# Two transformer blocks on one Trainium2 core: the modulation vectors computed on VectorE instead of GpSimd and TensorE

## The chip, the cores and the metric

One core of a Trainium2 chip (trn2) runs the whole program in one launch. The metric is the device time of one execution in microseconds. Five engines work side by side, each through its own queue in order: TensorE (PE, with its weight loads shown as PEld), VectorE (DVE), ScalarE (ACT), GpSimd (POOL) and SyncE (SP), which only issues DMAs here. They wait for one another by semaphores.

## The reference, cut to what matters

Two blocks, each of two layers. The first runs on 272 tokens (256 and 16 meta tokens), the second on 512 (256 and 256 of a context). In the second block every sublayer is wrapped by a modulation: a vector for each of two streams, made once from a condition by a matrix product, which shifts, scales and gates each sublayer.

```python
def ada_in(h, g, m, j):                       # m: the modulation of a layer and stream
    xn = rms_norm(h, g)
    return (xn * (1.0 + m[:, j, 1][:, None]) + m[:, j, 0][:, None]).astype(h.dtype)

def gated_residual(h, m, j, y, w):
    return h + (w * m[:, j, 2][:, None] * y).astype(h.dtype)
```

For each layer and each of two streams the vector has 9 x 1024 values: `silu(c) @ w_mod + b_mod`, with c of 1024 values, so 9216 outputs a layer, 144 tiles of 128 outputs in both layers. `w_mod` of both layers is 75 MB, read once.

## The kernel before, in words

All large products are cut in panels of weights, 128 x 1024 floats (512 KB), 632 of them, in one list that is walked in order. A panel lands in one of four slots of `raw` (SP, L370, issued when the panel four places back is used up), is split in a high part `whi` (ACT, L1078) and a low part `wlo` (DVE, L1642), and TensorE multiplies each of its eight 128 x 128 pieces three times (L484 to L486: high by high, low by high, high by low). `split` and `next_panel` do this on ACT and DVE: after each finished panel (`panel_done`) one further panel is split, three panels ahead of TensorE. The results go to PSUM banks 0 to 3 in turn, and `bank_free` gives them back.

Block 1 (layers 0 and 1): norm, input projection, attention of three kinds with panels between its steps as fillers, merge, a feed-forward of 32 panels in and 32 panels out. Layer 1 of it works on 256 columns. Block 2: a SwiGLU (44 panels in, 22 out), retention (16 panels of queries and keys, token tiles, heads, 16 panels out), SwiGLU, SwiGLU, neighbourhood attention, SwiGLU. Each sublayer ends in `residual`: 8 output tiles m = 0 to 7, each added to `h` by DVE (`update`), then a norm. Between residual and norm, called a boundary below, TensorE sums squares (L599, L606), ACT takes the root (L1122), DVE the reciprocal and four diagonal tiles (L1679, L1682), TensorE spreads them (L612), and DVE and ACT write the normed input chunk by chunk (L1719, L1142, L1708), which TensorE's first three tiles follow (L525, L526, L530).

The modulation is computed beside this in 36 groups of 512 outputs:

- POOL (`mod_group`, L389 to L437) reads the weights with the input dimension on the partitions. For a group it loads four pieces of 128 x 1024 (L436), multiplies each half by the condition's value of each partition (`tensor_scalar`, L400) and adds it up in `macc` (`tensor_tensor`, L402), 30 steps a group, each waiting for the one before. It then waits until TensorE has read `macc` (`mod_done`), and at four groups until the norm's low parts are written (`POOL_HOLD`).
- TensorE (`mod_group`, L504 to L512) sums `macc` over the partitions by 8 products with a tile of ones, of 64 columns each. It stands at fixed places in TensorE's program, given by the tables at L83 to L85: after a unit, after the spreads and after two heads of the stick-breaking attention; inside the residual, between panels of the feed-forwards, and in five boundaries (`mod_norm`), between L606 and L612.
- DVE (`mod_tiles`, L1741) adds the bias and writes `modv`, a bank of PSUM to each group.
- `modulations` turns the scale part into gains `gsc` and halves the gates.

POOL also stores the bias tables of the neighbourhood attention by column (L445), one after each of the last 16 groups but one, and later fills `bia` from them.

## Time and profile before

| | us |
|---|---|
| median of 3 runs | 3238.52 |
| lowest, highest | 3232.12, 3242.91 |
| span of the profiled execution | 3230.1 |
| PE busy | 3136.0 (97%) |
| DVE busy | 1724.8 (53%) |
| ACT busy | 1270.9 (39%) |
| POOL busy | 1950.4 (60%) |

The span runs from the first to the last instruction of the profiled execution. Its own time outside the span isn't recorded; the median of the runs shown is 8.4 us above the span. Busy time of PE hides its clock: a matmul at half clock counts as busy for longer.

### The profile page before, as it was taken

To read this page: it belongs to the slowest core of one execution; us is meant where nothing else is said; L and a number is where in the kernel's file an instruction comes from. 1 tells how busy PE (TensorE), PEld (TensorE's weight loads), DVE (VectorE), ACT (ScalarE), POOL (GpSimd) and SP (SyncE) were. 2 spreads that over 40 slices of the span, in tenths; PEclk is the share of its full clock that TensorE was granted. 3 is DMA by queue.
4 is the path that set the end of the run, shared out by engine and by line. 5 is a ranking of instruction groups with operands and counts; after the bars stand their busy time and mean duration, and the time that the engine had idled before them with its cause. 6 is when DMAs were issued, how large, how long until landed. Compare 5 with 4: busy or idle time off the path is not lost.

```text
span 3230.1 us, 48616 instructions
## 1 busy us (share of the span) xinstructions
PE 3136.0 (97%) x18046; PEld 2660.2 (82%) x18046; DVE 1724.8 (53%) x2409; ACT 1270.9 (39%) x2132; POOL 1950.4 (60%) x1285
## 2 busy tenths in 40 slices
PE   7999899999999999999999999999999999999998
PEld 6677899976779998888887777888888888886898
DVE  5665776655668865443435465544435443436554
ACT  4445555343555643222232443322223222235443
POOL 6658477514994975677567658678875777603000
PEclk9999999999999999999999999999999999999999
DMA  5323455632335663333443223334433443332354
GB/s 195 111 92 105 138 189 194 204 105 95 112 117 168 215 210 121 122 126 122 134 130 117 85 85 108 119 129 130 136 125 110 133 138 125 123 119 76 131 182 156
DMA packets 120280, 430.35 MB, mean 133 GB/s; under 512 B 13857, under 2 KB 17185, under 8 KB 119729
## 3 DMA queue, kind: packets, MB, share of 16 engines
q1 hardware_dynamic: 93632, 335.24, 31.7%
q0 software_dynamic: 24576, 86.46, 8.4%
q10 hardware_dynamic: 1904, 6.36, 0.5%
q8 instruction: 113, 1.85, 0.2%
q14 instruction: 55, 0.44, 0.1%
HBM read 426.95 MB, written 8.85 MB: 135 GB/s over the span
## 4 chain that ended last, share of the span: by engine, by line
PE 86%; POOL 5%; DVE 3%; ACT 2%; DMA 2%; issue 2%; ACTq 0%; DVEq 0%; SPq 0%; POOLq 0%
PE ps L484 22%; PE ps L486 21%; PE ps L485 21%; PE ps L511 2%; PE ps L581 2%; PE ps L582 2%; PE ps L583 2%; POOL macc L402 2%; DMA raw<-in_panels 2%; POOL modraw L400 2%; POOL mprod L400 1%; PE ps L525 1%; PE ps L530 1%; PE ps L526 1%; PE ps L986 1%
## 5 line engine op out<-in xcount | busy, mean ns | idle before, releaser
L1642 DVE TENSOR_TENSOR wlo<-raw,whi 128x1024 fp32r<-128x1024 f32 x632 | 856.0, 1355 | 914.6 <-ACT whi L1078 889.5
L1078 ACT ACTIVATE whi<-raw 128x1024 fp32r<-128x1024 f32 x632 | 668.4, 1058 | 1417.2 <-PE ps L486 901.2
L484 PE MATMUL ps<-xhi,whi 128*128 128x512 f32 (+2 forms) x2792 | 949.3, 340 | 3.1 <-DVE wlo L1642 2.5
L486 PE MATMUL ps<-xhi,wlo 128*128 128x512 f32 (+2 forms) x2792 | 934.6, 335 | 0.0
L485 PE MATMUL ps<-xlo,whi 128*128 128x512 f32 (+2 forms) x2792 | 933.7, 334 | 0.0
L484 PEld LDWEIGHTS ps<-xhi,whi 128*128 128x128 f32 x2792 | 531.8, 190 | 70.8 <-issue 14.8
L485 PEld LDWEIGHTS ps<-xlo,whi 128*128 128x128 f32 x2792 | 531.8, 190 | 51.8 <-issue 1.9
L486 PEld LDWEIGHTS ps<-xhi,wlo 128*128 128x128 f32 x2792 | 531.4, 190 | 50.2
L400 POOL TENSOR_SCALAR modraw<-modraw,cs 128x512 f32<-128x512 f32 x288 | 552.1, 1917 | 27.6
L400 POOL TENSOR_SCALAR macc<-modraw,cs 128x512 f32<-128x512 f32 x36 | 70.5, 1958 | 745.2 <-PE ps L511 602.5
L400 POOL TENSOR_SCALAR mprod<-modraw,cs 128x512 f32<-128x512 f32 x252 | 445.8, 1769 | 19.0 <-POOL macc L402 0.2
L402 POOL TENSOR_TENSOR macc<-macc,mprod 128x512 f32<-128x512 f32 x252 | 360.3, 1430 | 21.0
L402 POOL TENSOR_TENSOR macc<-macc,modraw 128x512 f32<-128x512 f32 x216 | 336.8, 1559 | 17.5
L484 PE MATMUL ps<-ghi,whi 128*128 128x512 f32 (+1 forms) x704 | 255.8, 363 | 0.0
L486 PE MATMUL ps<-ghi,wlo 128*128 128x512 f32 (+1 forms) x704 | 255.5, 363 | 0.0
L485 PE MATMUL ps<-glo,whi 128*128 128x512 f32 (+1 forms) x704 | 255.4, 363 | 0.0
L486 PEld LDWEIGHTS ps<-ghi,wlo 128*128 128x128 f32 x704 | 133.0, 189 | 20.6
L484 PEld LDWEIGHTS ps<-ghi,whi 128*128 128x128 f32 x704 | 133.0, 189 | 20.5
L485 PEld LDWEIGHTS ps<-glo,whi 128*128 128x128 f32 x704 | 133.0, 189 | 20.4
L2183 DVE TENSOR_TENSOR sq<-tmp,ps 128x512 f32<-128x512 f32 (+1 forms) x88 | 54.6, 620 | 175.1 <-PE ps L486 174.4
L484 PE MATMUL ps<-fhi,whi 128*128 128x272 f32 (+1 forms) x512 | 146.4, 286 | 0.3 <-DVE wlo L1642 0.3
L486 PE MATMUL ps<-fhi,wlo 128*128 128x272 f32 (+1 forms) x512 | 146.2, 286 | 0.0
(362 smaller groups left out, 4752.9 us busy)
## 6 DMA issues: line engine op xcount, KB each, us to landing
raw<-in_panels SPq DMA_DIRECT2D x632, 512.0 KB, 3.3
modraw<-in_mod POOLq DMA_DIRECT2D x144, 512.0 KB, 4.4
bias_by_column<-in_rpb POOLq DMA_DIRECT2D x16, 476.2 KB, 8.3
bia<-bias_by_column POOLq DMA_DIRECT2D x32, 96.0 KB, 2.6
rtab<-in_rtab ACTq DMA_DIRECT2D x2, 1312.0 KB, 7.4
wuq<-in_wuq ACTq DMA_DIRECT2D x2, 768.0 KB, 6.7
con<-in_con SPq DMA_DIRECT2D x1, 1345.5 KB, 13.7
h<-in_x SPq DMA_DIRECT2D x1, 1088.0 KB, 6.7
```

The source lines that it names most:

```text
L400: pool.tensor_scalar(out, a, b, None, op).then_inc(mod_step, 1)
L402: pool.tensor_tensor(out, a, b, op).then_inc(mod_step, 1)
L484: pe.matmul(out, w_hi, x_hi, start=start, stop=False)
L485: pe.matmul(out, w_hi, x_lo, start=False, stop=False)
L486: return pe.matmul(out, w_lo, x_hi, start=False, stop=stop)
L511: last = pe.matmul(bank(b, o, o + SUM_W), macc[:, s * 512 + j * P:s * 512 + (j + 1) * P], ones[:, 0:SUM_W], start=True, stop=True)
L581: pe.matmul(out, xh, wh(4 * kk, 512), start=(k == 0), stop=False)
L582: pe.matmul(out, xl, wh(4 * kk, 512), start=False, stop=False)
L583: last = pe.matmul(out, xh, wl(4 * kk, 512), start=False, stop=(k == NC - 1))
L1078: act.activation(whi[:, s * PW:(s + 1) * PW], raw[:, s * PW:(s + 1) * PW], ACT.Copy).then_inc(hi_split, 1)
L1642: dve.tensor_tensor(wlo[:, s * PW:(s + 1) * PW], raw[:, s * PW:(s + 1) * PW], whi[:, s * PW:(s + 1) * PW].bitcast(F32), ALU.subtract).then ...
L2183: dve.tensor_tensor(w_, v, bank(b, 0, T), ALU.mult).then_inc(bank_free[b], 1)
```

## The change

The weights of the modulation are laid out the other way round, with the output on the partitions: tile k holds 128 outputs and half a row, 512 of the 1024 input values (128 x 512, 256 KB, 288 such halves). The condition (both streams) is read to every partition (`cb`, 128 x 2048, a new DMA on SP), and ACT takes its silu there after the first norm. DVE multiplies a half by `cb` and sums along the row in one `tensor_tensor_reduce` for each stream; the second half starts from the sum of the first. After two tiles (four halves) DVE adds the bias and writes `modv`. POOL only issues the loads, two slots of 256 KB, each when the half in it is used up, and the bias tables' stores. TensorE's groups, their banks and the tables of places are gone.

The halves stand behind panels on DVE (`mod_half` after `next_panel`): 16 in each residual of block 1's feed-forward; in block 2 one behind each panel of three SwiGLUs (64 each), two behind each of the 16 panels of retention's queries and keys, one behind each of the 16 panels of its residual, and one behind each of the first 16 panels of the neighbourhood attention. `modulations` is now called just ahead of each norm, and the gates are halved ahead of the residual.

```diff
-AW = 23552
+AW = 24576
...
+            sp.dma_start(cb[:, :], t["cond"].broadcast_to([P, 2 * D])).then_inc(cond_in, 16)
...
+            n_halves = 2 * DEPTH * MODT
+            for k in range(n_halves):
+                s = k % 2
+                if k >= 2:
+
+                    pool.wait_ge(mod_step, 2 * (k - 1) + (k - 2) // 4)
+                pool.dma_start(modraw[:, s * MOD_W:(s + 1) * MOD_W], t["mod"][k, :, :]).then_inc(mod_landed[s], 16)
+                hh = (k - n_halves) // 8 + NH
+                if hh >= 0 and k % 8 == 7:
...
-                if mod:
-                    mod_group()
...
-                if c == 0:
-                    act.wait_ge(const_in, 32)
-                    act.activation(cs[:, :], par[:, P_C:P_C + 2 * NC], ACT.Silu).then_inc(silu_c, 1)
-                elif c == 4:
+                if c == 4:
                     split()
             for layer in range(DEPTH):
 
                 norm(T1, between=first_chunks if layer == 0 else None)
+                if layer == 0:
+                    act.wait_ge(cond_in, 16)
+                    act.activation(cb[:, :], cb[:, :], ACT.Silu).then_inc(silu_c, 1)
...
+            def mod_half():
+
+                j = mod_count.slot(4)
+                half, m = j % 2, j // 2
+                landed, done = lane.count(mod_landed[half]), lane.count(mod_step)
+                landed.add(16)
+                if mod_count.reg is None and mod_count.static == 0:
+                    dve.wait_ge(silu_c, 1)
+                dve.wait_ge(mod_landed[half], landed.value())
+                for s in range(2):
+                    w = modraw[:, half * MOD_W:(half + 1) * MOD_W]
+                    if done.reg is not None or done.static > 1:
+                        dve.wait_ge(mod_step, done.value(1))
+                    c = modsum[:, 2 * m + s:2 * m + s + 1]
+                    at = s * D + half * MOD_W
+                    dve.tensor_tensor_reduce(w if s else modprod[:, :], w, cb[:, at:at + MOD_W], 1.0, c if half else 0.0, ALU.mult, ALU.add,
+                                             modsum[:, 4 + 2 * m + s:5 + 2 * m + s] if half else c).then_inc(mod_step, 1)
+                    done.add(1)
...
+                        if mod and mod(m, e):
+                            mod_half()
...
+                residual(16, T2, add2(0, 1), mod=lambda m, e: True)
...
+                for i in range(16):
+                    next_panel()
+                    lane.tile.add()
+                    mod_half()
```

TensorE at the boundary from block 1 to block 2. Before:

```order
L486 MATMUL ps<-fhi,wlo 128x256
L599 MATMUL ps<-con,tmp 128x64 x4
L606 MATMUL ps<-con,sq 128x64 x4
L511 MATMUL ps<-con,macc 128x64 x8
L612 MATMUL ps<-sq,con 128x128 x4
L525 MATMUL ps<-xhi,whi 128x512
```

After, where L532 and L536 are the former L606 and L612:

```order
L428 MATMUL ps<-fhi,wlo 128x256
L525 MATMUL ps<-con,tmp 128x64 x4
L532 MATMUL ps<-con,sq 128x64 x4
L536 MATMUL ps<-sq,con 128x128 x4
L457 MATMUL ps<-xhi,whi 128x512
```

The eight products of the group are gone from between the sums of squares and the spreads; the same holds at four more boundaries.

DVE at the end of retention's residual, last output tile. Before:

```order
L1642 TENSOR_TENSOR wlo<-raw,whi 128x1024
L2166 SCALAR_TENSOR_TENSOR h<-ps,modv,h 128x256 x2
L1642 TENSOR_TENSOR wlo<-raw,whi 128x1024
L2208 SCALAR_TENSOR_TENSOR gsc<-modv,par 128x16
L2211 TENSOR_SCALAR modv<-modv 128x16
L1679 RECIPROCAL small<-small 128x4
```

After (`ISA` is the product with its sum, the `ISA` of 128x1 the read of the sum):

```order
L1654 ISA modprod,modsum<-modraw,cb,modsum 128x512
L1654 ISA modsum 128x1
L1654 ISA modraw,modsum<-modraw,cb,modsum 128x512
L1654 ISA modsum 128x1
L1662 TENSOR_TENSOR modv<-modsum,par 128x4
L2078 SCALAR_TENSOR_TENSOR h<-ps,modv,h 128x256 x2
L1547 TENSOR_TENSOR wlo<-raw,whi 128x1024
L2127 SCALAR_TENSOR_TENSOR gsc<-modv,par 128x16
```

One half, with the write of `modv`, now stands between the last panel and the last update of `h`.

DVE in the 16 panels of retention's queries and keys had 15 `wlo` in a row before. After:

```order
L1547 TENSOR_TENSOR wlo<-raw,whi 128x1024
L1654 ISA modprod,modsum<-modraw,cb 128x512
L1654 ISA modsum 128x1
L1654 ISA modraw,modsum<-modraw,cb 128x512
L1654 ISA modsum 128x1
L1654 ISA modprod,modsum<-modraw,cb,modsum 128x512
L1654 ISA modsum 128x1
L1654 ISA modraw,modsum<-modraw,cb,modsum 128x512
L1654 ISA modsum 128x1
L1547 TENSOR_TENSOR wlo<-raw,whi 128x1024
```

Two halves, four products with sums, stand between two `wlo`.

## Rows read from the trace of the kernel before

**Rows 1.** The page: busy us, share of the span and instructions of each engine
```profile
PE 3136.0 (97%) x18046; PEld 2660.2 (82%) x18046; DVE 1724.8 (53%) x2409; ACT 1270.9 (39%) x2132; POOL 1950.4 (60%) x1285
```

**Rows 2.** Groups by line, TensorE's modulation products: count, busy us, mean ns, idle before
```profile
L511 PE MATMUL ps<-con,macc 128*128 128x64 f32 x576 | 72.8, 282 | 4.5 <-POOL macc L402 3.8 <-ACT v L1511 0.7
```

**Rows 3.** The chain that ended last, in time: start us, us, what; some L511 pieces
```profile
919.95 2.94 PE ps L511 x16
...
1082.33 1.97 PE ps L511 x16
...
1152.97 1.73 PE ps L511 x16
...
1322.94 1.73 PE ps L511 x16
...
1390.05 1.73 PE ps L511 x16
```

**Rows 4.** Timeline of the boundary into block 2: start us, us, engine, line, idle before
```profile
1226.28 1.11 PE L606 MATMUL ps<-con,sq 128*128 128x64 f32 x8 [2.57 <-ACT sq L1116]
...
1228.09 0.88 DVE L1682 TENSOR_SCALAR sq<-con,small 128x128 f32<-128x128 f32 x4
...
1229.99 2.02 PE L612 MATMUL ps<-sq,con 128*128 128x128 f32 x8
...
1250.52 0.58 ACT L1460 ACTIVATE tmp<-ps 128x512 f32<-128x512 f32 x1
```

**Rows 5.** Timeline of the boundary into retention
```profile
1603.94 1.11 PE L606 MATMUL ps<-con,sq 128*128 128x64 f32 x8 [0.83 <-ACT sq L1116]
...
1605.69 0.87 DVE L1682 TENSOR_SCALAR sq<-con,small 128x128 f32<-128x128 f32 x4
1606.67 1.11 PE L612 MATMUL ps<-sq,con 128*128 128x128 f32 x8
...
1623.87 0.58 ACT L1485 ACTIVATE qk<-ps 128x512 f32<-128x512 f32 x1
```

**Rows 6.** Timeline of the boundary of layers 0 and 1, without a group
```profile
630.03 0.68 DVE L1682 TENSOR_SCALAR sq<-con,small 128x128 f32<-128x128 f32 x3
630.37 1.47 PE L612 MATMUL ps<-sq,con 128*128 128x128 f32 x6 [0.98 <-DVE sq L1682]
```

**Rows 7.** Windows of 2 us: busy PE, PEld, DVE, ACT, POOL; granted clock, DMA share, GB/s
```profile
632.00:634.00 2.00, 1.01 (x4) 1.04 (x5) 1.88 (x5) 0.96 (x3) 0.00 (x0) 0.50 0.66 256
...
1230.00:1232.00 2.00, 2.00 (x9) 1.72 (x9) 0.65 (x2) 0.28 (x1) 0.00 (x0) 0.50 0.00 0
...
1610.00:1612.00 2.00, 2.00 (x10) 1.67 (x9) 1.97 (x5) 0.91 (x2) 0.00 (x0) 1.00 0.01 5
```

**Rows 8.** DVE's groups by form in 2090 to 2430 us (POOL at work), then 3000 to 3230 (idle)
```profile
L1642 DVE TENSOR_TENSOR wlo<-raw,whi 128x1024 fp32r<-128x1024 f32 x62 | 86.6, 1397 | 132.1 <-ACT whi L1078 132.1
...
L1642 DVE TENSOR_TENSOR wlo<-raw,whi 128x1024 fp32r<-128x1024 f32 x71 | 87.0, 1225 | 87.2 <-ACT whi L1078 85.7 <-PE ps L486 1.4
```

**Rows 9.** Timeline of DVE: the only product-like operation with a sum, neighbourhood attention
```profile
2926.54 0.68 DVE L2372 CUSTOM_DVE_ANT_1 nsc<-ps,bia 128x512 f32<-128x512 f32 x1
2927.15 0.08 DVE L2372 DVE_READ_ACCUMULATOR2_ANT small<- 128x1 f32 x1
2927.15 0.69 DVE L2372 CUSTOM_DVE_ANT_1 nsc<-ps,bia 128x512 f32<-128x512 f32 x1
```

**Rows 10.** DMA issues: KB each, median us to landing; then the line L436 by itself
```profile
raw<-in_panels SPq DMA_DIRECT2D x632, 512.0 KB, 3.3
modraw<-in_mod POOLq DMA_DIRECT2D x144, 512.0 KB, 4.4
...
DMA to landing us min/median/max: 3.4/4.3/7.0
```

**Rows 11.** Waits of TensorE: us in total, times, longest
```profile
PE ps L765 <- DVE att L2062: 6.6, 4, 2.6
```

**Rows 12.** Timeline of the start: ACT's table load ahead of the silu
```profile
14.89 1.28 ACT L1179 ACT_TABLE_LOAD   x1
```

More of the change, by code:

```diff
@@ L502, in new_bank @@
                 return b
-            def mod_group():
-                b = new_bank()
-                lane.take(mod_step, MS)
-                for j in range(4):
-                    for s in range(2):
-                        o = (2 * j + s) * SUM_W
-                        last = pe.matmul(bank(b, o, o + SUM_W), macc[:, s * 512 + j * P:s * 512 + (j + 1) * P], ones[:, 0:SUM_W], start=True, stop=True)
-                last.then_inc(mod_done, 1)
             def first_tiles(T, w, count=FIRST, middle=None):
@@ L1305, in _ @@
                 filler(15)
-                lane.tile.add()
                 for hh in range(MH):
@@ L1409, in _ @@
                 lane.count(part_lo).add(NC)
-                residual(NC, T, mod_after=MOD_OUT, gain=layer * PL + P_LN2)
+                residual(NC, T, gain=layer * PL + P_LN2)
                 def relu(i):
@@ L1452, in shifts, with swiglu @@
                 return of
-            def swiglu(layer, j, T, norm_=None, mod=False, mod_after=()):
-                norm(T, shifts(layer, j, T), then=ACT.Silu, mod=mod)
+            def swiglu(layer, j, T):
+                norm(T, shifts(layer, j, T), then=ACT.Silu)
                 def pair(i):
@@ L1465, in pair @@
                     act.activation(col(ghi, i, T2, T), sq[:, (b // 2) * T2:(b // 2) * T2 + T], ACT.Copy).then_inc(part_hi, 1)
-                for part, (at, n) in enumerate(parts(2 * FF2, MOD_TILES2 if mod else ())):
-                    lane.tile.add(part > 0)
-                    with lane.loop(n // 4, [(lane.panel, 4), (lane.split, 4), (lane.tile, 4)]) as i:
-                        pair(i * 2 + at // 2)
-                        pair(i * 2 + (at // 2 + 1))
-                residual(FF2, T, norm_, mod_after)
+                with lane.loop(2 * FF2 // 4, [(lane.panel, 4), (lane.split, 4), (lane.tile, 4)]) as i:
+                    pair(i * 2)
+                    pair(i * 2 + 1)
+                residual(FF2, T)
             def block2():
                 lane.take(mod2_ready)
-                swiglu(0, 0, T2, None, True, MOD_FF2)
+                swiglu(0, 0, T2)
                 act.dma_start(rtab[:, :], t["rtab"]).then_inc(rtab_in, 16)
-                norm(T2, shifts(0, 1, T2), mod=True)
+                lane.take(mod2_ready)
+                norm(T2, shifts(0, 1, T2))
                 def qk_copy(i0):
@@ L1745, in residual @@
+            def residual(K, T, update, norm_=None, mod=None, between=None, gain=None):
                 norm_ = T if norm_ is None else norm_
@@ L2123, in _ @@
                 merged_lo(NC // 2 - 1)
-                residual(NC, T, add1, mod_after=MOD_OUT, gain=L + P_LN2)
+                residual(NC, T, add1, gain=L + P_LN2)
                 wait_tiles(lane)
@@ L2145, in _ @@
                 step(dve.tensor_copy(rs[:, 0:T], bank(5, 0, T)))
-                residual(FF1, T, add_folded, T1 if layer < DEPTH - 1 else T2, MOD_FF, between=decay_logs if layer == 0 else None)
+                residual(FF1, T, add_folded, T1 if layer < DEPTH - 1 else T2, mod=lambda m, e: m < NC - 1 and (e % 2 == 0 or (e == 1 and m < 2)), between=decay_logs if layer == 0 else None)
                 wait_tiles(lane)
@@ L2189, in pair @@
                     lane.count(part_lo).add()
-                for part, (at, n) in enumerate(parts(2 * FF2, MOD_TILES2 if mod else ())):
-                    if part:
-                        mod_tiles()
-                    with lane.loop(n // 4, [(lane.panel, 4), (lane.split, 4), (lane.tile, 4), (lane.count(part_hi), 2), (lane.count(part_lo), 2)]) as i:
-                        pair(i * 2 + at // 2)
-                        pair(i * 2 + (at // 2 + 1))
+                    if mod:
+                        mod_half()
@@ L2196, in swiglu @@
+                four = [(mod_count, 4), (lane.count(mod_landed[0]), 32), (lane.count(mod_landed[1]), 32), (lane.count(mod_step), 9)] if mod else []
+                with lane.loop(2 * FF2 // 4, [(lane.panel, 4), (lane.split, 4), (lane.tile, 4), (lane.count(part_hi), 2), (lane.count(part_lo), 2)] + four) as i:
+                    pair(i * 2)
+                    pair(i * 2 + 1)
                 lane.settle(part_lo)
-                residual(FF2, T, add2(layer, j), norm_, mod_after)
+                halves(layer, j)
```

253 lines of the change are left out of this document (81 added, 172 removed).

## The prediction, made blind

> **What bounds the kernel now.** I read the page first: TensorE is busy for 3136.0 of 3230.1 us, DVE for 1724.8, POOL for 1950.4 [rows 1]. So the end is set by TensorE's own queue nearly everywhere, and an edit is worth what it takes out of that queue or adds as a wait to it. Of TensorE's work I looked up the part that the change removes: 576 products at L511, busy for 72.8 us together, with 4.5 us of idle time in front, 3.8 of it for POOL's `macc` [rows 2]. POOL's 1950.4 us themselves cost next to nothing: it waits for TensorE, not the other way. The chain that ended last shows one group of L511 as one piece of 1.73 us at full clock, longer (up to 2.94) where the clock was low or POOL late; there are 36 such groups, 31 in line with other products and 5 at boundaries [rows 3]. The same rows give TensorE's pace: from 1322.94 to 1390.05 lie 12 panels and one group, so a panel of 512 columns takes 5.45 us; from 1082.33 to 1152.97 lie 24 panels of 256 columns, 2.86 us each [rows 3].
>
> **What is removed from TensorE, in line.** 29 of the 31 groups stand in a full queue: 29 x 1.73 = 50.2 us [rows 3]. The other two stand at the end of the stick-breaking attention of each layer, took 2.2 and 2.94 us and waited about 1.4 us each for POOL, 8.0 in all. A little behind them TensorE waits for the softmax of the differential attention on DVE (L765, up to 2.6 us a time, 6.6 in all [rows 11]), so arriving earlier partly lengthens that wait. Bounds 0 and 8.0; I take half, 4.0.
>
> **At the boundaries** the group stood where TensorE would wait for the diagonals anyway. Without a group the spreads start 0.34 us after the first diagonal was begun, 630.03 to 630.37 [rows 6]. With one, L612 started at 1229.99 where 1228.09 + 0.34 was possible [rows 4], 1.56 us late, and at 1606.67 where 1605.69 + 0.34 was possible [rows 5], 0.64 late. Five boundaries lie between 3.2 and 7.8 us; I take 5.0, the middle, since two had the long form.
>
> **DVE and POOL part company.** In the SwiGLU with POOL at work a `wlo` takes 1397 ns, at the end of the program with POOL idle 1225 [rows 8]. After the change POOL computes nothing until the neighbourhood attention. Where DVE hides behind TensorE that gives nothing; in attention, where TensorE waits for DVE's chains [rows 11], it may give 0 to 6.6 us. I take 2.0.
>
> Removed in all: 50.2 + 4.0 + 5.0 + 2.0 = 61.2 us.
>
> **What is added on DVE.** 288 halves of two products with a sum, each product followed by a read of the sum. The trace has one such operation, with one input in PSUM: the next starts 0.61 us after it, the read of 0.08 us inside that time [rows 9]. A half is then 2 x 0.61 and some 0.2 for the last read and the waits, 1.4 to 1.5 us; 288 of them 430 us. In a SwiGLU, a panel gives DVE 5.45 us, of which `wlo` takes 1.2, the product and the low part of a tile pair 0.7 a panel (two operations of 128 x 512 for two panels, 0.68 each as in [rows 9]), and the half 1.5: 3.4 of 5.45. With two halves behind a panel it is 1.2 + 3.0 = 4.2 of 5.45. In the first 8 panels of the neighbourhood attention it is 1.2 + 1.5 = 2.7 of 2.86, just enough; in block 1's residuals, two or three halves on four panels, about the same. Behind the waiting half on DVE stands the next `wlo`, and for that TensorE waits. The cover is the lead of three panels: at 2.86 us 8.6 us, less a panel's way of 3.3 for landing [rows 10], 1.2 for `whi` (twice the 0.58 of 512 columns [rows 4]) and 1.2 for `wlo`, leaves about 3 us; at 5.45 more. So the products are hidden, with bounds 0 and what the rivals below give; I take 1.0 for small stalls in the tight stretches.
>
> At one place there is no cover. In retention's residual the last half stands between the last panel and the last update of `h`, on the path to the norm: 1.4 us and the write of `modv` (0.1 to 0.2). **1.5 us**, once.
>
> **The loads.** A slot is filled again when its half is used up. A load of 512 KB from POOL lands after 3.4 to 7.0 us, median 4.3 [rows 10]; the new ones are 256 KB, so 4.3 is a cautious value. One half a panel at 5.45 us: two panels, 10.9 us, for 1.5 + 4.3. Two halves a panel: 5.8 for 5.45, a lag of 0.35 a panel, 5.6 us in 16 panels, mostly inside the lead. At 2.86: 5.8 for 5.72. Covered, by the 1.0 above. The bias stores stay behind loads of halves at the SwiGLU's pace and end with the last half, before the panels of values that come ahead of the first score with a bias; I count nothing.
>
> **The start.** The silu of `cb` on ACT is now 2048 columns wide: a table load of 1.28 [rows 12] and four times 0.58 [rows 4], 3.6 us behind the norm, just where ACT should split panel 3. TensorE has two panels of work then, so between 0 and 3.6 reach it; I take 1.2. The silu of 16 columns that goes had stood beside DVE's work.
>
> **The clock at the boundaries.** At the boundary into block 2, after an idle time of 2.57 us ahead of L606 [rows 4], the granted clock went to 0.50 (1.2 GHz); at the one into retention, with 0.83 idle [rows 5], it stayed at 1.00 (2.4 GHz) [rows 7]. From the spreads to the first evacuated tile it took 20.53 us there [rows 4] and 17.20 here [rows 5]: a fall costs 3.3 us. Of the five boundaries with a group three had fallen already; so had the one of layers 0 and 1, which has no group and only short gaps (clock 0.50 at 632 [rows 7]). After the change the two that held lose the group that filled their gap; the one behind retention's residual gets 1.5 us of idle time on top. I take both as falling: 6.6 us, bounds 0 and 6.6.
>
> **The sum.** 61.2 - 1.0 - 1.5 - 1.2 - 6.6 = 50.9 us less, a span of about 3179 instead of 3230.1. The profiled execution lies 8.4 us below the median of the runs shown, a distance that stays, so 3238.5 - 50.9 = 3187.6, rounded to **3187 us**, 1.6% faster.
>
> **Rivals.**
>
> *The gaps don't cost the clock and attention gains* (chance 0.18). No further fall (+6.6), the two late groups in full (+4.0), more relief of DVE in attention: 61 to 68 us less, about 3173. For it: the clock held at two of five; against: no boundary without a group held.
>
> *The product with a sum takes twice as long with both inputs in SBUF* (0.08). No row shows that form; `wlo`, with both in SBUF and no sum, runs at 1.2 ns an element [rows 8], the same as the summing form with one in PSUM [rows 9], which speaks against it. A half is then 2.7 us. Two a panel: 5.4 + 1.2 = 6.6 for 5.45, 1.2 x 16 = 18.4 us; at 2.86: 1.04 x 8 = 8.3; block 1's residuals some 7; the uncovered half 1.2; less about 12 for the lead of four stretches: 23 us lost, 3211. This is what a page of the Trainium skill would have: "Vector Engine (DVE) Microarchitecture Reference", section 7, says that the scalar-tensor-tensor shape loses half its throughput when both sources come from SBUF and aren't bf16, since no read port is left for the accumulator. I can't tell whether it holds for this operation, so it speaks against the change for 23 us only.
>
> *Attention takes back its groups* (0.08). Eight groups stand there; if TensorE waits for DVE and ACT right behind all of them, about 12 us more are lost and it is 3199.
>
> *The halves land late* (0.06), the case that ends slower. DVE waits in order for a load, the `wlo` behind it is late, and TensorE stands still. With L from issue to landing, a pair of slots turns in 1.5 + L. Lost: 16 (1.5 + L - 5.45) in the queries and keys, 10 times (1.5 + L - 5.72) in the neighbourhood panels and block 1's residuals, less 12 for the lead. At L = 7.0, the longest of before [rows 10], that is 65 us: 3252, slower than before. From L = 6.5 on it eats the whole gain. For it: these stretches carry the panels beside, at 2.86 us 512 KB each or 183 GB/s; against: median 4.3 for twice the size.
>
> *The change does nothing* isn't open: TensorE's 72.8 us of L511 are gone for certain; they could only come back as waits, as above.
>
> **Chances and range.** The forecast with its own spread, 3177 to 3198, 0.60; the fast rival 0.18; attention 0.08; double time 0.08; late halves 0.06, half of that beyond the old time. The range holds the forecast, attention, most of the fast rival and the double time: 3168 to 3212. About 0.3%, 10 us, is what a measurement of this kernel can tell from no change. Faster by more than that: 0.94; within it 0.02; slower 0.04.
>
> **What would show it.** No L511 and a TensorE busy time near 3080 us. At the five boundaries the spreads 0.34 us after the first diagonal, and a clock of 0.50 for 8 to 10 us at all of them. A product with a sum of 0.61 to 0.69 us (1.2 would be the second rival), DVE's busy time near 1930 us, that is 1724.8 and 576 x 0.65 more, less some 170 (632 `wlo` and the other forms with both inputs in SBUF, each up to 0.17 shorter [rows 8]). `wlo` near 1225 throughout. In the queries and keys and in the first neighbourhood panels, waits of DVE for the loads below 1 us. Wrong would be: waits of TensorE for `wlo` of more than 5 us in these stretches, or an unchanged clock at the boundaries with a gain above 60 us.

## The result, and the profile after

The changed kernel takes **3154.59 us** (median of 4 runs, 3153.55 to 3155.57) against 3239.43 us (4 runs, 3232.12 to 3242.91) for the kernel before on the same chip: a ratio of 0.9739, 95% interval 0.9722 to 0.9756. It is 2.6% faster, 84.8 us. The forecast was 3187 us with a range of 3168 to 3212: the right sign, and a gain that is two thirds larger than forecast. The page of the changed kernel, as [rows 1]:

```profile
span 3151.8 us, 48239 instructions
PE 3061.4 (97%) x17470; PEld 2586.3 (82%) x17470; DVE 1865.4 (59%) x3597; ACT 1272.4 (40%) x2132; POOL 204.6 (6%) x349
```

The 576 group products of [rows 2] are gone from TensorE, and POOL is down from 1950.4 to 204.6 us. DVE has 141 us more. The products by the tile that they write, half of all (the other half writes `modraw` and has the same durations), with DVE's waits ahead of them:

```profile
engine op xcount: duration ns min/median/max, first and last start us, forms
L1654 DVE CUSTOM_DVE_ANT_0 modprod<-modraw,cb x144: 680/684/694, 511.8 to 2815.1; 128x512 f32<-128x512 f32 x144
L1654 DVE CUSTOM_DVE_ANT_0 modprod<-modraw,cb,modsum x144: 742/746/752, 515.0 to 2823.9; 128x512 f32<-128x512 f32 x144
...
  DMA modraw<-in_mod: 31.0, 28
```

A product with both inputs in SBUF takes 0.68 us, as the nearest row of before with one input in PSUM did [rows 9]; where the sum is carried on from the first half of the row it takes 0.75. DVE waited 31.0 us in all for a half to land, 22.4 of them at 1570 to 1660 us, in retention's queries and keys, where two halves stand behind each panel (us in total, times, longest):

```profile
DVE modprod L1654 <- DMA modraw<-in_mod: 22.4, 20, 2.2
```

TensorE hardly felt it: all its waits for `wlo` at L426 in the whole run are 3.8 us. The loads, as [rows 10]:

```profile
raw<-in_panels SPq DMA_DIRECT2D x632, 512.0 KB, 3.5
modraw<-in_mod POOLq DMA_DIRECT2D x288, 256.0 KB, 3.0
```

And DVE in the SwiGLU at 2030 to 2370 us, as [rows 8]; `wlo` is down from 1397 to 1226 ns, the value that before had only with POOL idle:

```profile
L1547 DVE TENSOR_TENSOR wlo<-raw,whi 128x1024 fp32r<-128x1024 f32 x64 | 78.4, 1226 | 96.7 <-ACT whi L992 95.5 <-issue 1.0
```

**Where the 78.3 us of span went.** Both kernels issue the same 17,470 other products on TensorE in the same order, so each product of after can be set beside its twin of before, and the distance between them, read along the program, is a ledger of the gain. It jumps by 1.70 to 1.73 us at 25 of the 29 groups in line. At two, those behind the spreads of the latent attention (190.7 and 805.2 us before), it jumps by 0.5 only: TensorE then waits for DVE's `att` instead, 1.45 us each time. At two others it jumps by 2.9 and 2.7, since TensorE had also waited there before (0.9 us for POOL's sum, 0.7 for ScalarE). And there is one entry nobody had asked for:

| Entry (us of span, gain positive) | Forecast | Measured |
|---|---|---|
| 29 groups in line | 50.2 | 49.3 |
| 2 late groups of the stick-breaking attention | 4.0 | 7.7 |
| 5 groups at boundaries | 5.0 | 4.8 |
| Differential attention and merge, beside its groups | 2.0 | **17.4** |
| Small stalls | -1.0 | -1.1 |
| Uncovered half behind retention's residual | -1.5 | -1.5 |
| Start | -1.2 | +0.8 |
| Clock at the boundaries into retention and behind it | -6.6 | -5.2 |
| Wait for `wlo` in retention's rope | 0 | 2.0 |
| The rest: 0.06 to 0.13 us right behind each group in line (2.5 together), 0.7 more at the boundary ahead of neighbourhood attention, small pieces | 0 | 4.1 |
| Span | 50.9 | 78.3 |

At the boundary ahead of neighbourhood attention the clock was at 0.50 for 13.7 us before and 3.4 after, and that gave next to nothing: with the clock up TensorE waits there for DVE's `xlo`, 0.37 us at a time and once 0.85. The wait in the rope is DVE relieved of POOL once more: its twelve operations took 13 us before and 8 after, and a wait of 1.88 us for `wlo` went.

The other 6.5 us of the 84.8 are not in this ledger, which compares one execution of each kernel: the span profiled before lies 9.3 us below the median time of that kernel, the one profiled after 2.8 below. In the changed kernel and in e1 to e10 the time is 1.7 to 2.0 us above the span, so the profile of before caught a fast execution.

### The profile page after: what moved, and what is told of

Its sections match the earlier page's. It is cut to its first block and busy times, and to the rows that moved or that the text cites. A ratio compares the mean times of both kernels' runs of the same rounds, so it can differ in the third digit from the quotient of the medians.

```text
span 3151.8 us, 48239 instructions
## 1 busy us (share of the span) xinstructions
PE 3061.4 (97%) x17470; PEld 2586.3 (82%) x17470; DVE 1865.4 (59%) x3597; ACT 1272.4 (40%) x2132; POOL 204.6 (6%) x349
## 5 line engine op out<-in xcount | busy, mean ns | idle before, releaser
L1547 DVE TENSOR_TENSOR wlo<-raw,whi 128x1024 fp32r<-128x1024 f32 x632 | 773.5, 1224 | 730.5 <-ACT whi L992 694.6
L426 PE MATMUL ps<-xhi,whi 128*128 128x512 f32 (+2 forms) x2792 | 945.5, 339 | 4.3 <-DVE wlo L1547 3.8
L426 PEld LDWEIGHTS ps<-xhi,whi 128*128 128x128 f32 x2792 | 529.4, 190 | 73.1 <-issue 15.4
L384 POOL DMA_DIRECT2D modraw<-in_mod x288 | 155.1, 539 | 2643.6 <-DVE modsum L1654 2457.6
L426 PE MATMUL ps<-ghi,whi 128*128 128x512 f32 (+1 forms) x704 | 255.2, 362 | 0.0
L426 PEld LDWEIGHTS ps<-ghi,whi 128*128 128x128 f32 x704 | 132.9, 189 | 20.8
L426 PE MATMUL ps<-fhi,whi 128*128 128x272 f32 (+1 forms) x512 | 146.1, 285 | 0.1
L427 PE MATMUL ps<-flo,whi 128*128 128x272 f32 (+1 forms) x512 | 145.8, 285 | 0.0
L507 PE MATMUL ps<-whi,xhi 128*128 128x512 f32 (+1 forms) x288 | 116.5, 405 | 2.6 <-ACT qk L1392 1.8
L508 PE MATMUL ps<-whi,xlo 128*128 128x512 f32 (+1 forms) x288 | 114.6, 398 | 0.0
L509 PE MATMUL ps<-wlo,xhi 128*128 128x512 f32 (+1 forms) x288 | 114.5, 397 | 0.0
```

The lines of the kernel that those rows point to most:

```text
L384: pool.dma_start(modraw[:, s * MOD_W:(s + 1) * MOD_W], t["mod"][k, :, :]).then_inc(mod_landed[s], 16)
L426: pe.matmul(out, w_hi, x_hi, start=start, stop=False)
L427: pe.matmul(out, w_hi, x_lo, start=False, stop=False)
L507: pe.matmul(out, xh, wh(4 * kk, 512), start=(k == 0), stop=False)
L508: pe.matmul(out, xl, wh(4 * kk, 512), start=False, stop=False)
L509: last = pe.matmul(out, xh, wl(4 * kk, 512), start=False, stop=(k == NC - 1))
```

## The experiments

Ratios are to the kernel before on the same chip, with 95% intervals. Runs e1 to e4 shared their runs of before (3241.1 us), so did e5 to e8 (3241.2), and e9 and e10 (3241.4). The stretch that most of them are about is the differential attention with its merge, once in each layer of block 1, between the same two products of TensorE in every kernel. Windows over it: us, then busy time of PE, PEld, DVE, ACT and POOL (instructions), mean granted clock, DMA share, GB/s. The kernel before:

```profile
310.14:411.50 101.36, 92.81 (x650) 84.81 (x650) 71.69 (x140) 54.00 (x116) 52.06 (x34) 0.93 0.41 139
922.90:1021.20 98.30, 89.88 (x650) 82.08 (x651) 72.34 (x139) 53.21 (x116) 50.63 (x34) 0.92 0.43 140
```

The changed kernel:

```profile
301.24:394.34 93.10, 89.70 (x649) 82.72 (x648) 64.65 (x140) 54.68 (x118) 0.00 (x0) 0.96 0.39 128
891.08:980.21 89.13, 84.06 (x649) 77.06 (x648) 63.12 (x138) 53.37 (x118) 0.00 (x0) 0.98 0.40 134
```

8.26 and 9.17 us less, 17.4 together. TensorE's idle time (the length less PE's busy time) fell by 5.15 and 3.35 us, 8.5 together. Its busy time fell too, for the same products, since the clock was at 0.50 for 13.3 and 15.1 us of them before and for 6.8 and 3.4 after: 18.2 us less at half speed, 9.1 us less lost. 8.5 and 9.1 are 17.6, the whole of it. DVE was busy 7.0 and 9.2 us less for the same operations. By place, TensorE's idle time fell by 5.1 us at the products that transpose `att` (L765), by 2.5 where it waits for DVE's gates and by 1.1 where it waits for `mlo`; its waits for ScalarE did not shrink.

How steady is such a stretch? The second profile of the changed kernel (e10 below) has 91.24 and 90.82 us for the same two, 1.9 less and 1.7 more, by where the clock fell; the sum is 182.06 against 182.23. In e8, whose edit changes nothing up to the end of these stretches, the sum is 185.7. So 3 us of a sum can come with no edit at all, and before has one profile only.

**Theory A:** POOL's arithmetic had held up DVE, and DVE's chain is what TensorE waits for here. **Rival B:** POOL's loads of 512 KB did. **Rival C:** the groups did, by their banks and their places.

**e1 and e2: POOL's arithmetic put back.** Into the changed kernel, in the two stretches and in part of the attention ahead of them, POOL gets work on two spare tiles that nobody reads; e1 alternates these two, e2 has writes alone:

```
+            if i % 2: pool.tensor_tensor(spare[0], spare[0], spare[1], ALU.add)
+            else:     pool.tensor_scalar(spare[1], spare[0], 1.0, None, ALU.mult)
...
+            pool.memset(spare[i % 2], 0.0)
```

> The changed kernel, with idle work put on POOL in both attentions of block 1: 140 operations of 128 x 512 each that read a spare tile and write one (tensor_scalar and tensor_tensor in turn, as the old kernel had them), over the stretches in which POOL had worked before; nothing else is changed. Theory A, DVE's operations with two inputs in SBUF were held up by POOL's reads and TensorE waited for DVE in the differential attention: the two stretches (310 to 413 and 923 to 1023 us before) get back most of the 17 us that they gained, the span rises by 12 to 20 us, wlo's mean in these stretches goes from 1225 to near 1400 ns, and half-clock time of TensorE there goes from 10 towards 28 us. Theory B, the loads of the modulation had disturbed the panels: no change (within 3 us). Theory C, the groups on TensorE cost more than their 1.73 us in the attention: no change.

> The changed kernel, with POOL kept busy in the same places by 420 memsets of 128 x 512 each, which write SBUF and read nothing. Theory A in the narrow form (POOL's reads hold DVE up): within 3 us of the changed kernel, wlo stays near 1225 ns. Theory A in the wide form (any work of POOL): slower by 10 us or more, like the run with reads. Theories B and C: no change.

e1 took 3177.86 us (0.9803, 0.9776 to 0.9829), e2 3163.3 us (0.9750, 0.9724 to 0.9775). That is 23.3 and 8.7 us more than the changed kernel; 12 to 20 were expected of e1, and e2 lies between its two forms of theory A. The windows of e1, then of e2:

```profile
302.69:402.31 99.62, 91.74 (x649) 84.05 (x648) 73.11 (x140) 54.54 (x118) 46.62 (x29) 0.93 0.36 121
902.17:998.59 96.42, 86.95 (x649) 78.82 (x648) 71.72 (x139) 53.10 (x118) 50.68 (x33) 0.95 0.37 124
```

```profile
301.87:398.67 96.80, 91.23 (x650) 83.78 (x649) 68.11 (x140) 54.64 (x118) 50.92 (x96) 0.95 0.38 125
892.77:985.41 92.64, 85.77 (x650) 78.17 (x648) 66.45 (x138) 53.07 (x118) 53.73 (x102) 0.96 0.39 129
```

With reads 13.8 of the 17.4 us are back, with writes alone 7.2. Which operations of DVE are hit, by form, in the stretch of layer 0; first the kernel before, then the changed kernel, then e1, then e2:

```profile
L2058 DVE TENSOR_SCALAR att<-att,small 128x144 f32<-128x144 f32 x4 | 2.6, 639 | 0.1
L2062 DVE SCALAR_TENSOR_TENSOR att<-att,small 128x144 f32<-128x144 f32 x4 | 2.1, 524 | 0.1
```

```profile
L1977 DVE SCALAR_TENSOR_TENSOR att<-att,small 128x144 f32<-128x144 f32 x4 | 1.5, 369 | 0.1
L1973 DVE TENSOR_SCALAR att<-att,small 128x144 f32<-128x144 f32 x4 | 1.2, 295 | 0.1
```

```profile
L1999 DVE TENSOR_SCALAR att<-att,small 128x144 f32<-128x144 f32 x4 | 4.8, 1196 | 0.1
L2003 DVE SCALAR_TENSOR_TENSOR att<-att,small 128x144 f32<-128x144 f32 x4 | 2.6, 640 | 0.1
```

```profile
L1996 DVE TENSOR_SCALAR att<-att,small 128x144 f32<-128x144 f32 x4 | 2.5, 613 | 0.1
L2000 DVE SCALAR_TENSOR_TENSOR att<-att,small 128x144 f32<-128x144 f32 x4 | 1.5, 368 | 0.1
```

A `tensor_scalar` of 144 columns takes 295 ns with POOL idle, 613 beside POOL's writes and 1196 beside its reads; the operation with two inputs in SBUF takes 369, 368 and 640: only reads hold it. These are small instructions in a serial chain, so a wait of some 0.3 to 0.9 us is a multiple of what they do, and TensorE's wait for that chain (the products that transpose `att`) goes in layer 0 from 0.7 us in the changed kernel to 5.0 in e1 and 2.6 in e2; it was 3.2 before. This agrees with the Trainium skill, "SBUF — State Buffer", section "Who interferes with whom": a DVE instruction with two inputs in SBUF contends with a GpSimd instruction that reads SBUF and not with one that only writes, and the forms that enter a two-port mode, `tensor_scalar` among them, contend with both.

e1 is no exact copy of before: at these operations and at this wait its POOL is the heavier load, and the 13.8 us may say more than POOL's reads cost before. Nor is every instruction beside POOL held: nine of the 22 `wlo` in layer 0's stretch of before, also with two inputs in SBUF, ran wholly or partly beside POOL's arithmetic and took 1204 to 1226 ns, while in e1 two of six took 1715 and 2243. The expected rise of their mean to near 1400 ns came out as 1288.

**e3: loads put back.** POOL issues 27 more loads of 512 KB into a spare tile in each layer, one for two panels, and computes nothing.

> The changed kernel with 27 loads of 512 KB more in each attention of block 1, issued by POOL every second panel into a spare tile (14 MB each, somewhat more than the modulation's loads there before). Theory B: the panels land later, whi and wlo too, and the span rises by 10 to 17 us. Theories A and C: within 3 us.

3156.38 us (0.9732, 0.9707 to 0.9757), no different from the changed kernel. Windows of e3:

```profile
303.13:396.19 93.06, 89.57 (x649) 82.68 (x648) 64.52 (x139) 53.73 (x117) 5.83 (x11) 0.96 0.54 190
890.02:979.54 89.52, 84.17 (x650) 77.08 (x648) 63.28 (x139) 53.13 (x118) 5.83 (x11) 0.98 0.55 195
```

190 GB/s in place of 128 and the same 93.1 us, and 89.5 against 89.1 in layer 1: rival B is out.

**e4: the other way round.** The kernel before, with POOL's arithmetic taken out but for one step of 8 columns for each quarter of a group. Loads, groups on TensorE and DVE's reads of them stay.

```
-                    for k in range(2): ...        # 30 steps of 512 columns a group
+                    step(macc[:, 8 * q:8 * q + 8], w[0][:, 0:8], c[0][0], ALU.mult)
```

> The kernel before, with POOL's arithmetic left out: one product of 128 x 8 for each load instead of the products and sums, so the modulation vectors aren't computed; all loads and all groups on TensorE stay. Theory A: 17 to 22 us faster than before (about 3218), the gain in the differential attentions of block 1 and some in retention, and about 62 us slower than the changed kernel. Theories B and C: as before within 5 us, apart from the 3 us for which TensorE had waited for POOL.

3223.63 us (0.9932, 0.9904 to 0.9960). Windows:

```profile
304.24:401.74 97.50, 91.11 (x649) 83.37 (x649) 64.33 (x139) 53.97 (x116) 4.47 (x8) 0.95 0.43 141
907.64:1000.52 92.88, 85.56 (x650) 77.95 (x649) 63.01 (x138) 52.66 (x116) 4.08 (x8) 0.96 0.45 146
```

DVE is as free as in the changed kernel (64.33 and 63.01 us), and 9.3 of the 17.4 us are gained with the groups still in place. So POOL's arithmetic accounts for 9.3 us when it is taken from before and for up to 13.8 when it is put into the changed kernel, in both directions more than half, and behind e4 8.1 us need something more. The expectation for the whole run held: 17.5 us less than before, 17 to 22 expected. e4 also prices what is left between it and the changed kernel: 3223.6 to 3154.6, 69 us, of which the ledger puts 61.8 at the groups.

**e5: one group of e4 moved.** In e4 TensorE waited at the entry of layer 0's stretch, right behind the late stick group, and went through it at half clock. e5 is e4 with that group three heads earlier:

```
-MOD_UNIT, MOD_STICK = (6,), (0, 7)
+MOD_UNIT, MOD_STICK = (6,), (0, 4)
```

> The kernel of run e4 (the kernel before with GpSimd's arithmetic left out, so the modulation isn't computed; 36 groups on TensorE, the loads and VectorE's reads of the groups stay) with one thing changed: in each layer of block 1 the group behind the eighth stick-breaking head, right ahead of the differential attention, stands behind the fifth head instead. The number of groups is the same. In e4 TensorE waited 1.43 us for a ScalarE write at the entry to the differential attention of layer 0, its granted clock fell to 0.50 for 6.8 us right after, and the stretch from there to the merge was some 4 us longer in each layer than in the changed kernel. Theory (that group holds up the entry, and the gap is what brings the clock down): the wait there shrinks below 0.8 us, as in the changed kernel (0.72), the clock stays at 1.00, and the time falls by 3 to 8 us against e4: 3216 to 3221 us. Rival (the rest of e4 has to do with VectorE's missing products or with GpSimd's loads): the wait and the time stay, 3223 to 3225 us.

3222.29 us (0.9945, 0.9928 to 0.9963): no change in the sum that can be told, where 3 to 8 us less than e4 were expected. TensorE's waits at that entry, of e4 and then of e5, and the clock right behind:

```profile
PE ps L768 <- ACT att L1359: 1.4, 1, 1.4
PE ps L756 <- DVE att L2053: 0.8, 1, 0.8
...
320.00:326.00 6.00, 6.00 (x34) 4.78 (x32) 3.38 (x13) 2.78 (x14) 0.00 (x0) 0.50 0.01 4
```

```profile
PE ps L756 <- DVE att L2053: 0.8, 1, 0.8
...
324.00:330.00 6.00, 6.00 (x43) 5.46 (x43) 4.41 (x16) 2.20 (x3) 0.00 (x0) 1.00 0.25 87
```

What the theory said of this place happened: the wait of 1.4 us is gone, the clock stays at 1.00, the stretch of layer 0 is 3.1 us shorter. In layer 1 the wait at the same entry went from 2.46 us to 0.77 and the stretch is 1.5 us shorter, but the wait for `wlo` right behind the merge grew from 2.5 to 3.9 us and took that back. And in e5's trace the clock was at 0.50 for 6.8 us near 190 us, where e4's held, which cost 3.0 us. So of the 8.1 us the place of the late groups accounts for some 4.7, read from one profile of each kernel. The last 3.4 stay open; e8's sum lies as far above the changed kernel's with no edit in these stretches.

**e6: every product on DVE twice.** How much cover did the halves have?

```
+                    dve.tensor_tensor_reduce(modprod, w, cb[...], 1.0, 0.0, ALU.mult, ALU.add, <the column that the real product overwrites>)
```

> The changed kernel with every product on VectorE issued twice (the first of a pair is overwritten by the second): a half takes four products of 0.69 to 0.75 us in place of two, so VectorE gets some 576 x 0.77 = 443 us more work, all of it in the stages where the halves stand, and nothing else moves. Theory of the prediction (half a row behind each panel leaves cover, and a half of twice the time costs a little at each place where VectorE runs close to TensorE): 15 to 35 us more than the changed kernel, 3170 to 3190 us. Rival (cover is ample): up to 5 us more, 3155 to 3160 us. Rival (VectorE was about to bound these stages): 60 us and more, above 3215 us.

3217.14 us (0.9927, 0.9905 to 0.9950): 62.6 us more than the changed kernel, nearly twice the most that the theory of the forecast allowed (15 to 35) and the value of the last rival. DVE has 418 us more (2283.4). The waits for `wlo` are back in TensorE's rows:

```profile
L426 PE MATMUL ps<-xhi,whi 128*128 128x512 f32 (+2 forms) x2792 | 948.5, 340 | 28.0 <-DVE wlo L1547 27.5
L426 PE MATMUL ps<-fhi,whi 128*128 128x272 f32 (+1 forms) x512 | 148.9, 291 | 11.4 <-DVE wlo L1547 10.5
...
1600.00:1690.00 90.00, 72.28 (x276) 55.23 (x276) 81.17 (x207) 18.52 (x24) 12.36 (x23) 0.92 0.42 140
```

The first of these waits was 3.8 us in the changed kernel. Set beside its twin as above, TensorE loses 33.7 us in retention's queries and keys and the few panels right behind them (1570 to 1670 us of the changed kernel), where two halves stand behind each panel and DVE is busy for 81 of 90 us; 16.9 in block 1's feed-forward residuals (two or three halves on four panels), 5.9 in the first panels of neighbourhood attention, the rest in small pieces. In the three SwiGLUs, with one half behind each panel, it loses next to nothing. So the halves, 1.4 us each in the trace, are hidden; at 3.0 they are hidden only where a panel of 512 columns carries one.

**e7: the uncovered half moved.** The last half of retention's residual goes from behind the last panel to behind the first.

```
-                residual(16, T2, add2(0, 1), mod=lambda m, e: True)
+                residual(16, T2, add2(0, 1), mod=lambda m, e: 2 if m == e == 0 else 0 if m == NC - 1 and e == 1 else 1)
```

> The changed kernel with one half of 288 moved: the last one of retention's residual, behind its last panel, stands behind its first panel, beside the one that is there. Theory of the prediction (that half lies uncovered between the last panel and the last residual add, and the gap it makes is paid again by the granted clock, which is 0.50 for 6.8 us after it): the gap of 2.33 us ahead of the last sum of squares at 2004 us shrinks to some 0.8 us as at the other boundaries, and the time falls by 1.5 us; if the shorter gap is enough to keep the clock at 1.00, by 4 us. 3150.5 to 3153 us. Rival (the last residual add waits for TensorE's last tile anyway): no change, 3154.6 us.

3157.99 us (0.9737, 0.9717 to 0.9757): not to be told from the changed kernel; the 3150.5 to 3153 expected did not come. The timeline shows the edit at work. The boundary in the changed kernel, then in e7 (start us, us, engine, line, in brackets the idle time before it):

```profile
2000.60 0.75 DVE L1654 CUSTOM_DVE_ANT_0 modprod<-modraw,cb,modsum 128x512 f32<-128x512 f32 x1 [1.83 <-PE ps L428]
...
2002.15 0.87 DVE L2078 SCALAR_TENSOR_TENSOR h<-ps,modv,h 128x256 f32<-128x256 f32 x2
...
2003.73 1.10 PE L532 MATMUL ps<-con,sq 128*128 128x64 f32 x8 [2.33 <-ACT sq L1030]
...
2005.85 2.06 PE L536 MATMUL ps<-sq,con 128*128 128x128 f32 x8 [1.02 <-DVE sq L1587]
```

```profile
2004.42 0.88 DVE L2078 SCALAR_TENSOR_TENSOR h<-ps,modv,h 128x256 f32<-128x256 f32 x2 [1.52 <-PE ps L428]
...
2006.05 1.10 PE L532 MATMUL ps<-con,sq 128*128 128x64 f32 x8 [0.83 <-ACT sq L1030]
...
2008.17 1.16 PE L536 MATMUL ps<-sq,con 128*128 128x128 f32 x8 [1.02 <-DVE sq L1587]
```

2.33 us of idle time became 0.83, exactly the 1.5. The clock still fell to 0.50 for 6.8 us behind it, with waits of 0.83, 1.02 and 1.20 us in a row. It did so at 1549 and 2372 us too, but not at 2740 us: behind the same three waits it stayed at 1.00 there, in both profiles of the changed kernel, until 2753 to 2757 us. So these waits go with the fall at most boundaries, not at every one. Retention takes 2.3 us less in this trace; other stretches of half clock (115.4 us in all, 103.4 in the changed kernel's profile) took it back.

**e8: work for TensorE in the boundary's waits.**

```
+            def keep(n, T):
+                for _ in range(n if T != T1 else 0):
+                    pe.matmul(bank(4, 0, P), ones, ones, start=True, stop=True)
...
+                keep(2, T)      # ahead of the last sums of squares
...
+                keep(2, T)      # ahead of the spreads
...
+                keep(3, T)      # behind them
```

> The changed kernel with seven small products on TensorE at each boundary of block 2 whose result nobody reads (128 columns of the ones matrix, 0.34 us each as the spreads of the norm take): two ahead of the last sums of squares, two ahead of the spreads, three behind them, where TensorE now waits 0.83, 1.02 and 1.20 us in a row. Theory (the waits cost twice, once as idle time and once as a granted clock of 0.50 for 3.4 to 10.2 us behind them): with TensorE at work in the waits the clock stays at 1.00 there and each of the five boundaries that show it gives back about 2.6 us, which is what the clock cost at the boundaries at 1604 and 2068 us of the trace before: 8 to 15 us less than the changed kernel, 3140 to 3147 us. Rival (the clock falls at a boundary whatever TensorE does in the waits, and the extra products delay the spreads): 0 to 3 us more, 3154 to 3158 us.

3149.69 us (0.9721, 0.9701 to 0.9741). That is 4.9 us less than the changed kernel's first runs and 2.2 less than its second ones (e10), with intervals that overlap, so the runs alone don't show a gain; 3140 to 3147 were expected. Windows of 2 us in the boundaries at 1554, 2007 and 2376 us of the changed kernel, then of e8, as [rows 7]:

```profile
1553.00:1555.00 2.00, 0.80 (x3) 0.53 (x3) 1.63 (x6) 1.61 (x4) 0.00 (x0) 0.50 0.49 199
2007.00:2009.00 2.00, 0.91 (x5) 0.61 (x3) 1.53 (x4) 1.04 (x3) 0.00 (x0) 0.50 0.00 0
2376.00:2378.00 2.00, 1.24 (x3) 1.08 (x4) 1.97 (x6) 1.31 (x3) 0.00 (x0) 0.50 0.00 0
```

```profile
1554.00:1556.00 2.00, 1.48 (x13) 1.29 (x13) 1.11 (x6) 0.26 (x1) 0.00 (x0) 1.00 1.01 406
2007.00:2009.00 2.00, 1.80 (x14) 1.64 (x14) 1.78 (x7) 1.38 (x3) 0.00 (x0) 1.00 0.04 8
2372.00:2374.00 2.00, 1.48 (x13) 1.30 (x12) 1.60 (x7) 1.36 (x3) 0.00 (x0) 1.00 0.00 0
```

The clock held at every boundary from 1192 us to 3144 us. From the first product of block 2 to the end it takes 1955.7 us against 1964.9, 9.1 less: 2.0 to 2.2 for each SwiGLU and 2.8 for retention, read at their places. In the last stage two stretches of 0.50 went too and nothing was gained. Each extra product is two records 0.11 us apart, at most 0.17, so it took 0.22 to 0.28 us where 0.34 were expected, and it delayed nothing. Up to the first product of block 2 the profiled execution was 5.3 us longer, though the edit adds products only at the last boundary there; 3.3 of them are the clock (68.1 us at 0.50 against 61.6).

**e9 and e10: the sum of both, and the partner.** e9 has e7's move and e8's products, also at the boundaries of block 1 (three ahead of the spreads, ten where block 1 ends) and four behind the up-projections of the latent attention (MLA). e10 is the changed kernel again.

> The changed kernel with the moved half of run e7 (the last half of retention's residual stands behind its first panel) and the idle-time products of run e8, now at the boundaries of block 1 too, three in place of two ahead of the spreads, ten ahead of the last sums of squares where block 1 ends (run e8 shows 3.26 us of waiting there, and a clock of 0.50 for 6.8 us behind it) and four behind the MLA up-projections (1.45 us of waiting at 189 and 782 us, 0.50 for 6.8 us). In run e8 the clock stayed at 1.00 at every boundary of block 2 from 1192 us on. Theory (a TensorE that has work in its waits keeps its clock, wherever the wait is): the 0.50 stretches at 188, 608, 782 and 1185 us go too, worth up to 3.4 us less 0.7 to 1.4 us of waiting each, and 1.5 us come from the moved half: 5 to 11 us less than run e8, 3139 to 3145 us. Rival (the waits of block 1 are ended by chains that the extra products delay, and the clock falls elsewhere instead): 3148 to 3152 us, as e8.

> The changed kernel once more, as the partner of run e9 on the same chip: 3154.6 us within 3 us. How far its stretches of half clock stand elsewhere than in its first profile shows what the clock's own scatter is worth: every theory expects the same sum, and 0.50 behind the same five boundaries of block 2.

e9: **3137.93 us** (3134.56 to 3143.05; 0.9691, 0.9671 to 0.9711). e10: 3151.88 us (3150.18 to 3157.30; 0.9735, 0.9715 to 0.9754). 14 us less on the same chip, 0.44%; the ranges of their runs do not touch, and 3139 to 3145 us were expected of e9. The page of e9:

```profile
span 3132.8 us, 48591 instructions
PE 3064.1 (98%) x17646; PEld 2591.1 (83%) x17646; DVE 1866.7 (60%) x3597; ACT 1272.5 (41%) x2132; POOL 204.4 (7%) x349
```

TensorE's time at half clock is 50.5 us against 96.5 in e10 and 103.4 in the first profile of the same kernel. From the first product of block 2 to the end it is 1952.2 us, 12.8 less than e10's 1965.0. The stretch of 0.50 at 603 us became two half as long. Those at 186 and 777 us stayed. The wait of 1.45 us in front of these two is not the one behind the up-projections, as the expectation had it: it lies between the spreads of the scales and the first transposes of the latent attention, where no extra product stands. It is the wait that took the place of two groups in the ledger. So that part was not tested; at the end of block 1 the clock held as expected. e9 makes three changes at once; the runs show their sum, and the share of each is read from places in the trace.

## Why the prediction was right and wrong

**Right: TensorE's queue sets the end, and a group in line is worth 1.73 us.** 29 groups gave 49.3 us (50.2 forecast), the five at boundaries 4.8 (5.0), and at all five the spreads now start 0.34 us after the first diagonal. No L511 is left, and TensorE's busy time is 3061.4 us (3080 forecast). That 29 groups come so close to 29 x 1.73 is in part luck: two gave 1.2 us less each, as the rival "Attention takes back its groups" had it for eight, and two gave about 1 us more.

**Right: the products are hidden.** 0.68 and 0.75 us a product, 1.4 a half, small stalls of 1.1 us (1.0). DVE's 1865 us were forecast as 1930: the products and their reads keep DVE busy for 392.6 us, so its other work was relieved by some 250 us and not 170. A third of that is `wlo`, as forecast; other forms with both inputs in SBUF fell by far more than the 0.17 us each of the forecast, the low part `glo` (128x512) from 1160 to 684 ns. One sign was missed: DVE's waits for the loads in the queries and keys were to stay below 1 us, and reached 2.2. The rival by which the product takes twice the time is out: 0.68 us with both inputs in SBUF. The rule of the Trainium skill behind it ("Vector Engine (DVE) Microarchitecture Reference", section 7) doesn't show in this operation, nor in the trace's `scalar_tensor_tensor` itself: with both inputs in SBUF it takes 748 ns for 512 columns, with one in PSUM 683. But e6 shows that the price which the forecast gave that rival was too low: 23 us at 2.7 us a half, while 3.0 us cost 62.6. It had 18.4 for retention's queries and keys, 8.3 for the neighbourhood panels and 7 for block 1's residuals, less 12 for the lead of three panels; e6 shows 33.7, 5.9 and 16.9. In the queries and keys its own sum of work per panel, 2 x 3.0 + 1.2 - 5.45, gives 28 us for 16 panels, with no lead taken off. Nothing in e6 shows the lead as a saving.

**Right: the uncovered half.** -1.5 us on the ledger, and e7 takes exactly that away from the wait. The halves landed after 3.0 us in the median (4.3 assumed), and where they did come late, in the queries and keys, the lead of three panels hid it.

**Wrong: "DVE and POOL part company", 2.0 us, bounds 0 and 6.6.** It is 17.4. This one term is 15.4 of the 27.4 us by which the span was missed. Behind it stands the premise of the first paragraph, that POOL's arithmetic costs next to nothing because TensorE is not waiting for POOL: it was paid through DVE. Two steps of the sizing failed. First, the relief was sized from the large `wlo` [rows 8], 12% shorter, and 2.0 us were taken. In layer 0's attention `wlo` didn't change at all (1220 ns both times), while small forms halved: 639 to 295 ns for the one shown above. In layer 1 that form was free before (297 ns) and others were held, the 16x16 `tensor_scalar` at 660 ns against 216. The wait at L765 [rows 11] gave 5.1 us by itself, within the bound of 6.6, and the waits for DVE's gates and `mlo` gave 3.6 more, which no row of the forecast had. Second, the clock was counted as a loss at the boundaries but never as a gain in attention: TensorE was at 2.4 GHz for 18.2 us more of the same products, 9.1 us. POOL's arithmetic put back returns 13.8 of the 17.4 us (e1), taken out of the kernel before it gains 9.3 without moving a product (e4), and e3 excludes the loads. That POOL's arithmetic is the larger part of the cause is shown; the late groups' place accounts for some 4.7 us more (e5, in one profile), and the last 3.4 stay open.

**Wrong by half: the late groups** (4.0, measured 3.39 and 4.29). TensorE's later wait at L765 didn't grow by the earlier arrival: with POOL idle it is 0.8 us in each layer with the groups in place (e4) and 0.7 to 0.8 without them.

**The clock at the boundaries.** The direction was right, the clock fell at both boundaries where it had held, 2.6 us each and not 3.3. But it was to be at 0.50 for 8 to 10 us at all five, and was so for 10.2 us at one and 6.8 at three; at the fifth it held through the boundary and fell for 3.4 us some 12 us behind it. The start gained 0.8 where 1.2 were to be lost. Retention's rope gave 2.0 us, which belongs to the term above: TensorE waited there for a DVE that POOL held up.

**The fast rival** had attention's gain and the late groups in full, but its first condition, no further fall of the clock, did not hold, and at 3173 us it didn't reach the result either. 5.6 us more come from the distance between profiled span and median, 8.4 us at the time of the forecast and taken as lasting; it is 2.8 for the changed kernel. Only some 1.8 of it lasts; the rest was the luck of which execution was profiled.

## What to carry to other kernels

An engine that is never waited for can still cost: before calling GpSimd's work free, compare the durations of VectorE's *small* operations, form by form, with GpSimd busy and idle, in the stage where TensorE waits on VectorE. Count the clock on both sides of the sum: here 8.5 us less of idle time came with 9.1 us of clock. It is no fixed rate: from e1 to the changed kernel it is 8.9 and 4.9, and in layer 1 of e5 1.7 and nothing. And where TensorE must wait for a short chain, a few products whose result nobody reads can hold its clock for next to nothing: 9.1 us of block 2 in e8, by its trace.

## What the runs showed of the hardware

- GpSimd's plain writes were enough to double a `tensor_scalar` on VectorE (295 to 613 ns), with reads in between it took four times as long (1196 ns); a two-input operation of the same size went from 369 to 640 ns, with reads only. Not every instruction beside GpSimd is held: nine `wlo` in attention took 1204 to 1226 ns beside it, as without it.
- Behind a row of waits of 0.83, 1.02 and 1.20 us, with little work between, TensorE went from 2.4 to 1.2 GHz for 6.8 us at 1549 and 2372 us, and not at 2740 us. With seven extra products of 0.22 to 0.28 us in and around them (waits of 0.33, 0.52 and 0.54 us left, once 1.83 in place of the first) it didn't fall once in 1950 us (e8).
- One and the same kernel had 103.4 and 96.5 us at half clock in two profiles, with spans of 3151.8 and 3148.4 us: an effect of 3 us is below what one profile can tell. Read at its place it is firmer, but a stretch of 93.1 us in the one profile was 91.2 in the other.
- A product with a sum takes 0.68 us when it starts from a constant and 0.75 us when it carries on a sum held in SBUF, for the same 512 columns.
